# Crossing the second pair of each first matrix, and adding the first sum of two pairs per later group on VectorE

## The chip, the cores and the metric

One core of a Trainium2 chip runs the kernel. The metric is the device time of one execution in microseconds. Before the change the median of three runs is 1181.12 us (1180.35 to 1185.26).

## What is computed

The reference is a two-layer encoder on 512 tokens of width 1024, with 16 learned tokens put in front (528 in all). What matters here is the MLP that ends each layer:

```python
def sq_relu_mlp(y, w_up, w_down):
    u = y @ w_up                                  # 1024 -> 4096
    return jnp.square(jax.nn.relu(u)) @ w_down    # 4096 -> 1024

for i in range(DEPTH):                            # DEPTH = 2
    y = rmsnorm(h, norm_gains[i, 0])
    y = mlstm_mixer(y, ...) if i % 2 == 0 else diff_attention(y, ...)
    h = h + y
    h = h + sq_relu_mlp(rmsnorm(h, norm_gains[i, 1]), mlp_w_up[i], mlp_w_down[i])
h = rmsnorm(h, final_gain)
```

Everything is float32. The MLP of layer 0 works on 528 tokens, that of layer 1 on 512.

## The kernel before

Activations lie transposed in SBUF, features on the 128 partitions and tokens along the row. Each float32 factor is split in a hi part (ScalarE copies it to the type of TensorE's operands) and a lo part (VectorE subtracts the hi part from the original), and each product is three matmuls: hi x hi, hi x lo, lo x hi.

The MLP's 4096 inner features are cut in four groups. A group has eight *pairs*; a pair is 256 output columns of a weight matrix, loaded as one transfer of 1 MB to `raw[:, i % 2]` by SyncE. Pairs 0 to 3 of a group are columns of `w_up` (their output is relu'd, squared and kept in `ah`, `al`), pairs 4 to 7 are columns of `w_down`. So i counts 0 to 31 in a layer.

A *plain* pair is two blocks of 128 columns, each with eight slices of the inner dimension: 96 matmuls of 264 columns in layer 0, 48 of 512 in layer 1. A *crossed* pair is a two-by-two block product with seven products instead of eight (Winograd's form). The weights' forms are S1 = A21 + A22, S2 = S1 - A11, S3 = A22 - S2, S4 = A12 - S2; the tokens' forms are kept in `th`, `tl`, made once at the start of a layer's MLP by `forms_hi` (ScalarE) and `forms_lo` (VectorE). The seven products A11, A12, S1, S2, S4, S3, A22 take 12 matmuls each. In between ScalarE copies the results of A11, S1 and S2 out of PSUM (`snap` P1, P5, U2), since their banks are added to by later products, and VectorE adds them back in two sums (`total` C22 and C1). S2's product waits for the copy P1, S4's for P5, S3's for U2, A22's for C22. `pe_order` writes the order of the products: the last product of a pair, A22, comes after A11 and S1 of the next one.

`crossed(i)` says which pairs are crossed. With PLAIN = 2, pairs 0 and 1 of the first matrix are plain, all other pairs of the first matrix and all `w_up` pairs of the later groups are crossed, and so are the last three `w_down` pairs of all groups but the last.

S1 needs a sum of two quarters of `raw`. GpSimd makes it (`weight_sum`, L741) by a DMA of 256 KB that reads the quarter from HBM again and accumulates it on the one in `raw`, after the 1 MB load has landed. The forms S2, S3, S4 are three VectorE instructions on 512 columns (`form`, L1734); their hi part is `form_hi`, their lo part `form_lo` (L1741); hi and lo parts of what is taken from `raw` as it is are `natural_hi` and `natural_lo` (L1747) in crossed pairs, `plain_hi` and `plain_lo` (L1686) in plain ones, with m = 0 for the first half and m = 1 for the second, which holds S1 and A22.

At the start of the MLP VectorE also refines the norm's factor (`refine_factor`, L1809 to L1811), and scales the residual in four pieces (`scale_residual`, L1801), which GpSimd saves to HBM (`h_sum`), since the squares overwrite `h`. `squares` is on ScalarE (L1116, L1117), the lo part of its result, `act_lo`, on VectorE (L1771).

Every engine's order is written out by hand in a loop over i; all of them take their work in order, and wait on semaphores that count what has been done. `READY`, `DONE`, `COPIED`, `ADDED` are tables of these counts. SyncE loads pair i when the lo part m = 1 of pair i - 2 is made (L626).

Of the kernel before, what the change touches and what calls it, by code (L numbers as in the profile page):

```python
# [72 lines left out]
PLAIN = 2  # L73
# [18 lines left out]
def sent_down(i):  # L92

    return 0 <= i < PAIRS - 8 and i % 8 >= 4

# [25 lines left out]
def counted(things):  # L121
# [7 lines left out]
RANK = counted(i for i in range(PAIRS) if crossed(i))  # L129
# [6 lines left out]
N_DONE, N_READY, N_TAKEN, N_OUT, N_CROSSED, N_COPIED, N_ADDED, N_SENT = (  # L136
    len(x) for x in (DONE, READY, TAKEN, SENT_OUT, RANK, COPIED, ADDED, SENT))
# [97 lines left out]
def program(nc, a, out):  # L235
    with ExitStack() as ctx:
# [275 lines left out]
        def raw_summed(layer, i):  # L512

            crosses = [k for k in range(i % 2, PAIRS, 2) if crossed(k)]
            return m_sum[i % 2], 16 * (len(crosses) * layer + crosses.index(i) + 1)
# [47 lines left out]
        def _(sp):  # L563
# [96 lines left out]
        def _(pool):  # L660
# [69 lines left out]
            def residuals(layer):  # L730
# [18 lines left out]
                for q in range(4):  # L749
                    if q % 2 == 0:  # L750
                        weight_sum(PLAIN + q // 2)
                    pool.wait_ge(h_scaled, FACTOR * layer + q + 3)
                    pool.dma_start(h_sum[2 * q:2 * q + 2, :, t0:T].rearrange("k p t -> p k t"),
                                   h[:, 2 * q:2 * q + 2, t0:T]).then_inc(h_saved[q // 2], 16)
                for q in range(2):
                    pool.wait_ge(h_saved[q], 32 * (layer + 1))
                for i in range(PAIRS - 7):
                    if sent_down(i):
                        send_sum(i, 0)
                        send_sum(i, 1)  # L760
                    if i + 3 > PLAIN + 1 and crossed(i + 3):
                        weight_sum(i + 3)
# [44 lines left out]
        def _(act):  # L807
# [249 lines left out]
            def mlp(layer, spans):  # L1057
                t0, w = mlp_shape(layer)
                mid = t0 + w
                items, ranks, norm = layer * N_DONE, layer * N_CROSSED, 2 * layer + 1  # L1060
                copies, adds = layer * N_COPIED, layer * N_ADDED

                def form_hi(i, group):

                    act.wait_ge(s_made, 3 * (ranks + RANK[i] - 1) + (2 if group == "S23" else 3))
                    act.wait_ge(m_done, items + last_use(i, "S3" if group == "S23" else "S4"))
                    rows = slice(8, 16) if group == "S23" else slice(16, 20)
                    copy(hi[1 - i % 2][:, rows, :], lof[1 - i % 2][:, rows, :]).then_inc(m_hi, 1)

                def natural_hi(i, m):  # L1070

                    act.wait_ge(*(raw_summed if m else raw_landed)(layer, i))
                    act.wait_ge(m_done, items + last_use(i, "A22" if m else "A12"))
                    copy(hi[1 - i % 2][:, slots(i, m), :], raw[:, i % 2, :, P * m:P * m + P]).then_inc(m_hi, 1)
# [26 lines left out]
                def squares(i, m):  # L1101
# [3 lines left out]
                    if i > 0:  # L1105
                        positive(i, m)
# [56 lines left out]
                for i in range(PAIRS):  # L1163
                    if i == 0:
                        plain_hi(layer, 1, 0)
                        plain_hi(layer, 1, 1)
# [10 lines left out]
                    if begins:  # L1177
                        snap(i, "P1")
                        if i == PLAIN:
                            squares(1, 0)  # L1180
                        else:
# [9 lines left out]
                    if i == PLAIN:  # L1191
                        squares(1, 1)
                    if first_down:
                        block_hi(i, "A22")
                    if crossed(i + 1) and not first_down and i != PLAIN:
                        natural_hi(i + 1, 1)
                    if crossed(i) and is_up(i) and not begins:
                        snap(i, "U2")
# [3 lines left out]
                    if i > 1 and not in_tail(layer, i - 1) and not sent_down(i - 1) and not (sent_down(i) and i % 8 == 4) and not begins and not last_row:  # L1202
# [25 lines left out]
                    if i == 1:  # L1228
                        squares(0, 0)
                        squares(0, 1)  # L1230
                    if i >= PAIRS - 4 and not in_tail(layer, i):
                        finish(i, 0)
                    if first_down:
                        snap(i + 1, "P1")
                        snap(i + 1, "P5")
                        finish(i, 0)
                    elif crossed(i):
                        if i == PLAIN:
# [196 lines left out]
        def _(dve):  # L1435
# [280 lines left out]
            def mlp(layer, spans):  # L1716
                t0, w = mlp_shape(layer)
                mid = t0 + w
                items, ranks, norm = layer * N_DONE, layer * N_CROSSED, 2 * layer + 1
                copies, adds, t_in = layer * N_COPIED, layer * N_ADDED, spans[0][0]  # L1720

                def form(i, name, after):

                    made = 3 * (ranks + RANK[i] - 1)
# [5 lines left out]
                    if name == "S2":  # L1730
                        dve.wait_ge(*raw_summed(layer, i))
                    wait(dve, s_made, after and made + after)
                    dve.wait_ge(m_done, items + last_use(i, name))
                    V.tensor_tensor(f[:, out_rows, :], x, y, ALU.subtract).then_inc(s_made, 1)  # L1734

                def form_lo(i, group):

                    dve.wait_ge(s_made, 3 * (ranks + RANK[i]))
# [14 lines left out]
                def total(i, name):  # L1753
# [6 lines left out]
                    else:  # L1760
                        dve.wait_ge(m_done, items + DONE[i, "S3"])
                        dve.wait_ge(p_copied, copies + COPIED[i, "P5"])
                        dve.wait_ge(*freed(layer, i - 2, 1))
# [40 lines left out]
                def refine_factor():  # L1804

                    made, ms, r = FACTOR * layer + 1, ab[1][:, t_in:T], rb[:, t_in:T]
# [37 lines left out]
                for i in range(PAIRS):  # L1844
                    if i == 0:
                        plain_lo(layer, 1, 0)
                        plain_lo(layer, 1, 1)
                        refine_factor()
                        for n in range(4):
                            forms_lo(n)  # L1850
                        scale_residual(0)
                        scale_residual(1)
# [8 lines left out]
                    if crossed(i + 1):  # L1861
# [10 lines left out]
                    if crossed(i + 1):  # L1872
# [261 lines left out]
        def _(pe):  # L2134
# [228 lines left out]
            def mlp(layer, spans):  # L2363
                t0, w = mlp_shape(layer)
                mid = t0 + w
                items, ranks, norm = layer * N_DONE, layer * N_CROSSED, 2 * layer + 1
# [21 lines left out]
                def plain_waits(i, m):  # L2388
# [4 lines left out]
                    else:  # L2393

                        pe.wait_ge(evac, u_out + (5 if (i, m) == (0, 0) else 8))
                        if (i, m) == (1, 1):
                            pe.wait_ge(ln_done, norm + 1)

                def product(i, name):
# [8 lines left out]
                    if name in ("A11", "S1", "A12"):  # L2408
                        pe.wait_ge(*freed(layer, i - 2, int(name == "A11")))
                    elif name == "A22":  # L2410
# [303 lines left out]
```

## Time and profile before

| | |
|---|---|
| median of three runs | 1181.12 us |
| profiled execution | 1185.41 us |
| its span, first to last instruction | 1183.6 us |
| TensorE busy | 1170.5 us, 99% |
| VectorE busy | 947.8 us, 80% |
| ScalarE busy | 794.7 us, 67% |
| GpSimd busy | 176.7 us, 15% |
| granted TensorE clock | 0.999 of full speed |
| moved by DMA | 143.83 MB, mean 122 GB/s |

The MLP of layer 0 runs from about 251 to 590 us of the span, that of layer 1 from about 837 us to near the end. Busy times are those of instructions; a wait shows as idle time before an instruction, with what ended it.

### The profile page before, as it was taken

What the parts mean: (1) busy time and instruction counts of PE and PEld (TensorE: products, weight loads), DVE (VectorE), ACT (ScalarE), POOL (GpSimd) and SP (SyncE); (2) the same over time, 40 slices, a digit from 0 to 9 for tenths busy, and PEclk for the clock granted to TensorE, in tenths of its full rate; (3) what the DMA queues carried; (4) which work ended last, traced back from release to release, by engine and by line L of the source; (5) the groups of instructions that cost most, each with busy time, mean ns of one, the idle gap of its engine ahead of it and who ended that gap; (6) DMA issues with size and microseconds to landing.
All of it is one profiled execution on the core that took longest, in us unless ns stands there. A gap on an engine that the chain in (4) does not pass through costs nothing.

```text
span 1183.6 us, 23240 instructions
## 1 busy us (share of the span) xinstructions
PE 1170.5 (99%) x8881; PEld 1125.1 (95%) x8881; DVE 947.8 (80%) x1441; ACT 794.7 (67%) x1401; POOL 176.7 (15%) x215
## 2 busy tenths in 40 slices
PE   9999999999999999999999999999999999999998
PEld 8999999999999999999999999987799899999987
DVE  6889888778977878775578889887988788797764
ACT  5777877756667667666357887887576676766753
POOL 3221120001220220222020000000103103113100
PEclk9999999999999999999999999999999999999999
DMA  7343332335694793884132122213458748759722
GB/s 180 95 104 95 89 98 90 93 100 163 146 187 125 137 195 99 175 198 141 55 96 66 55 71 71 89 37 92 129 157 166 167 102 181 156 135 185 195 75 72
DMA packets 176634, 143.83 MB, mean 122 GB/s; under 512 B 23913, under 2 KB 167329, under 8 KB 176545
## 3 DMA queue, kind: packets, MB, share of 16 engines
q1 hardware_dynamic: 141600, 104.93, 30.1%
q0 software_dynamic: 34816, 37.59, 18.6%
q8 instruction: 60, 0.98, 0.3%
q14 instruction: 30, 0.24, 0.1%
q10 hardware_dynamic: 128, 0.09, 0.0%
HBM read 123.42 MB, written 19.17 MB: 120 GB/s over the span
## 4 chain that ended last, share of the span: by engine, by line
PE 76%; issue 17%; DMA 4%; DVE 2%; ACT 1%; POOL 1%; DVEq 0%; POOLq 0%; ACTq 0%
PE ps L2433 36%; PE ps L2148 18%; PE ps L2383 14%; DMA raw<-in_mlp_w_up_dram 3%; PE ps L2652 2%; PE ps L2203 1%; PE ps L2221 1%; PE ps L2335 0%; PE ps L2300 0%; DMA meta_in<-in_meta_tokens_dram 0%; PE ps L2289 0%; DVE lo L1747 0%; DVE blocks_f L1787 0%; ACT wh L809 0%; POOL qm L794 0%
## 5 line engine op out<-in xcount | busy, mean ns | idle before, releaser
L809 ACT ACTIVATE hi<-raw 128x1024 fp32r<-128x1024 f32 x128 | 133.5, 1050 | 44.3 <-PE ps L2383 20.0
L2148 PE MATMUL ps<-yh,wh 128*128 128x264 f32 (+1 forms) x704 | 160.6, 302 | 0.0
L2148 PE MATMUL ps<-yl,wh 128*128 128x264 f32 (+1 forms) x704 | 155.3, 295 | 0.0
L2148 PE MATMUL ps<-yh,wl 128*128 128x264 f32 (+1 forms) x704 | 155.3, 295 | 0.0
L2433 PE MATMUL ps<-th,hi 128*128 128x264 f32 (+1 forms) x448 | 127.3, 284 | 3.7 <-ACT pu L809 2.8
L2433 PE MATMUL ps<-tl,hi 128*128 128x264 f32 (+1 forms) x448 | 126.5, 282 | 0.0
L2433 PE MATMUL ps<-th,lo 128*128 128x264 f32 (+1 forms) x448 | 126.5, 282 | 0.0
L1747 DVE TENSOR_TENSOR lo<-raw,hi 128x1024 fp32r<-128x1024 f32 x92 | 112.2, 1220 | 5.4 <-ACT hi L809 4.9
L2433 PE MATMUL ps<-yl,hi 128*128 128x264 f32 (+1 forms) x408 | 115.7, 284 | 0.0
L2433 PE MATMUL ps<-yh,hi 128*128 128x264 f32 (+1 forms) x408 | 115.3, 283 | 0.0
L2433 PE MATMUL ps<-yh,lo 128*128 128x264 f32 (+1 forms) x408 | 115.1, 282 | 0.0
L2148 PEld LDWEIGHTS ps<-yh,wh 128*128 128x128 f32 x704 | 112.0, 189 | 2.9 <-DVE yl L1448 0.4
L2148 PEld LDWEIGHTS ps<-yh,wl 128*128 128x128 f32 x704 | 111.1, 188 | 2.8
L2148 PEld LDWEIGHTS ps<-yl,wh 128*128 128x128 f32 x704 | 111.3, 188 | 1.6
L1741 DVE TENSOR_TENSOR lo<-lof,hi 128x1024 fp32r<-128x1024 f32 x92 | 86.9, 952 | 4.0 <-ACT hi L809 4.0
L2433 PEld LDWEIGHTS ps<-th,hi 128*128 128x128 f32 x448 | 84.4, 188 | 5.3 <-ACT pu L809 3.4
L809 ACT ACTIVATE hi<-lof 128x1024 fp32r<-128x1024 f32 x92 | 73.6, 836 | 21.0 <-DVE lof L1734 20.2
L1441 DVE TENSOR_TENSOR wl<-raw,wh 128x1024 fp32r<-128x1024 f32 x64 | 78.2, 1222 | 9.4 <-ACT wh L809 8.0
L2433 PEld LDWEIGHTS ps<-tl,hi 128*128 128x128 f32 x448 | 84.4, 188 | 0.0
L2433 PEld LDWEIGHTS ps<-th,lo 128*128 128x128 f32 x448 | 84.3, 188 | 0.0
L2433 PE MATMUL ps<-al,hi 128*128 128x264 f32 (+1 forms) x288 | 81.6, 283 | 0.0
L2433 PE MATMUL ps<-ah,hi 128*128 128x264 f32 (+1 forms) x288 | 81.5, 283 | 0.0
(332 smaller groups left out, 3463.4 us busy)
## 6 DMA issues: line engine op xcount, KB each, us to landing
raw<-in_mlp_w_up_dram SPq DMA_DIRECT2D x32, 1024.0 KB, 6.5
raw<-in_mlp_w_down_dram SPq DMA_DIRECT2D x32, 1024.0 KB, 5.5
raw<-in_diff_w_in_dram SPq DMA_DIRECT2D x24, 512.0 KB, 3.7
raw<-in_mlstm_w_in_dram SPq DMA_DIRECT2D x16, 512.0 KB, 4.4
raw<-in_mlp_w_up_dram POOLq DMA_DIRECT2D x28, 256.0 KB, 7.2
h_sum<-abuf POOLq DMA_DIRECT2D x24, 264.0 KB, 5.8
h_sum<-abuf POOLq DMA_DIRECT2D x24, 256.0 KB, 6.5
raw<-in_mlp_w_down_dram POOLq DMA_DIRECT2D x18, 256.0 KB, 5.0
```

The lines of the kernel that those rows point to most:

```text
L809: return nc.scalar.activation(o, i, ACT.Copy, scale=scale)
L1441: V.tensor_tensor(wl[:, k, :, :], raw[:, k // 2, :, P * (k % 2):P * (k % 2) + P], wh[:, k, :, :].bitcast(F32), ALU.subtract).then_inc(spli ...
L1741: V.tensor_tensor(lo[1 - i % 2][:, rows, :], lof[1 - i % 2][:, rows, :], hi[1 - i % 2][:, rows, :].bitcast(F32), ALU.subtract).then_inc(m_ ...
L1747: V.tensor_tensor(lo[1 - i % 2][:, slots(i, m), :], raw[:, i % 2, :, P * m:P * m + P], hi[1 - i % 2][:, slots(i, m), :].bitcast(F32), ALU. ...
L2148: last = mm(ps[:, bank + s, 0:w_], w[:, slot, kb, :], m[:, kb, t0:t0 + w_], start=(kb == 0 and n == 0), stop=(kb == CB - 1 and n == 2))
L2203: last = mm(ps[:, b, c:c + t1 - t0], what(j), p, start=(b not in seen), stop=(n == 1 and i == len(passes) - 1))
L2221: last = mm(ps[0:rows, b, c:c + t1 - t0], ks[par][:, s0:s0 + rows], q[:, t0:t1], start=(m == 0), stop=(m == 1))
L2383: last = mm(ps[:, b + s, 0:cw], x[half][:, 20 * m + kb, :], y[:, kb, c0:c0 + cw], start=(kb == 0 and n == 0), stop=(kb == CB - 1 and n == 2))
L2433: last = mm(ps[:, bank, 0:w], x[1 - i % 2][:, at, :], y, start=(kb == 0 and n == 0 and name in ("A11", "S1", "A12")), stop=(kb == 3 and n ...
L2652: last = mm(ps[:, j % 2, 0:XH], x[half][:, 20 * m + kb, :], y[:, kb, c0:c0 + XH], start=(kb == 0 and n == 0), stop=(kb == CB - 1 and n == 2))
```

## The change

PLAIN becomes 1: pair 1 of the first matrix is crossed as well. In pairs 0 and 1 of the later groups (i = 8, 9, 16, 17, 24, 25) VectorE adds the first sum itself (`own_sum`), and `weight_sum` is left out for them. The counts on the semaphore of the forms become a table, MADE. The order of the work at the start is rewritten on ScalarE and VectorE. Cut to its core:

```diff
-PLAIN = 2
+PLAIN = 1
+def summed_here(i):
+    return crossed(i) and i >= 8 and i % 8 < 2
-RANK = counted(i for i in range(PAIRS) if crossed(i))
+MADE = counted((i, n) for i in range(PAIRS) if crossed(i) for n in ("S1", "S2", "S3", "S4") if n != "S1" or summed_here(i))
 # SyncE, the load of pair i
-    sp.wait_ge(m_lo, layer * N_READY + READY[i - 2, "S1A22" if crossed(i - 2) else 1])
+    sp.wait_ge(m_lo, layer * N_READY + READY[i - 2, ("S23" if i - 2 == PLAIN + 1 else "S1A22") if crossed(i - 2) else 1])
 # GpSimd
 for q in range(4):
-    if q % 2 == 0:
-        weight_sum(PLAIN + q // 2)
-    pool.wait_ge(h_scaled, FACTOR * layer + q + 3)
+    if q == 0:
+        weight_sum(1)
+        weight_sum(2)
+    if q == 2:
+        weight_sum(3)
+    pool.wait_ge(h_scaled, FACTOR * layer + q + 1)
...
-        if i + 3 > PLAIN + 1 and crossed(i + 3):
+        if i + 3 > 3 and crossed(i + 3) and not summed_here(i + 3):
             weight_sum(i + 3)
 # ScalarE, loop over i
 if i == 0:
-    plain_hi(layer, 1, 0)
-    plain_hi(layer, 1, 1)
+    natural_hi(1, 0)
     norm_factor(norm, spans)
...
-if i == 1:
-    squares(0, 0)
-    squares(0, 1)
...
+elif i == PLAIN:
+    snap(i + 1, "P1")
+    snap(i + 1, "P5")
+    squares(0, 0)
+    squares(0, 1)
+    snap(i + 1, "U2")
+    positive(1, 0)
+    positive(1, 1)
+    natural_hi(i + 2, 1)
+    squares(1, 0)
+    squares(1, 1)
 elif crossed(i):
-    if i == PLAIN:
+    finish(i, 0)
+    if crossed(i + 1):
         snap(i + 1, "P1")
-    finish(i, 0)
-    if crossed(i + 1) and i != PLAIN:
-        snap(i + 1, "P1")
-    if crossed(i + 1):
         snap(i + 1, "P5")
 # VectorE
+def own_sum(i):
+    dve.wait_ge(*raw_landed(layer, i))
+    s1 = raw[:, i % 2, first_k(i), P:2 * P]
+    V.tensor_tensor(s1, s1, raw[:, i % 2, second_k(i), P:2 * P], ALU.add).then_inc(s_made, 1)
...
 if i == 0:
-    plain_lo(layer, 1, 0)
-    plain_lo(layer, 1, 1)
-    refine_factor()
+    natural_lo(1, 0)
+    form(1, "S2")
+    form(1, "S3")
+    form(1, "S4")
     for n in range(4):
         forms_lo(n)
-    scale_residual(0)
-    scale_residual(1)
...
-if crossed(i + 1):
+if crossed(i + 1) and i != PLAIN:
     natural_lo(i + 1, 1)
...
-if crossed(i + 1):
+if crossed(i + 1) and i != PLAIN:
     form_lo(i + 1, "S23")
...
 if i == PLAIN:
-    for n in range(4):
-        act_lo(n // 2, n % 2)
-elif i > 1 and is_up(i - 1) and not sent_down(i):
+    form_lo(i + 1, "S23")
+if i > 1 and is_up(i - 1) and not sent_down(i):
     act_lo(i - 1, 1)
...
+if i == 1:
+    scale_residual(2)
+    scale_residual(3)
...
 if crossed(i + 2):
+    if i == 0:
+        scale_residual(0)
+        scale_residual(1)
     if not (sent_down(i) and i % 8 == DOWN_FROM - 1):
         natural_lo(i + 2, 0)
-    form(i + 2, "S2", 0)
-    form(i + 2, "S3", 1)
-    form(i + 2, "S4", 1)
     if i == 0:
-        scale_residual(2)
-        scale_residual(3)
+        natural_lo(2, 1)
+    if summed_here(i + 2):
+        own_sum(i + 2)
+    form(i + 2, "S2")
+    form(i + 2, "S3")
+    form(i + 2, "S4")
+    if i == 1:
+        act_lo(0, 0)
+        act_lo(0, 1)
+        refine_factor()
```

So on VectorE the order from the start of the MLP to the second lo part of pair 3 is: lo (1,0), forms of pair 1, four `tl`, lo (1,1), both form lo parts of pair 1, two scalings, lo (2,0), lo (2,1), forms of pair 2, C22 and C1 of pair 1, both form lo parts of pair 2, two scalings, lo (3,0), forms of pair 3, `al` of pair 0 twice, the factor, lo (3,1). After it come `al` (1,0), the first form lo part of pair 3, C22 and C1 of pair 2. On ScalarE a pair's first two squares now stand before the next pair's P1 from pair 2 on.

## Rows read from the trace of the kernel before

**Rows 1.** The page's busy times, TensorE: busy, share of span, instructions.

```profile
PE 1170.5 (99%) x8881; PEld 1125.1 (95%) x8881; DVE 947.8 (80%) x1441; ACT 794.7 (67%) x1401; POOL 176.7 (15%) x215
```

**Rows 2.** Waits of TensorE over the span: us in total, times, longest us.

```profile
PE ps L2433 <- ACT pu L809: 2.8, 2, 2.1
...
PE ps L2433 <- DVE lo L1747: 0.6, 1, 0.6
```

**Rows 3.** The chain of waits: start us, us, what, instructions.

```profile
257.73 17.53 PE ps L2383 x144
275.26 20.45 PE ps L2433 x168
...
503.71 8.74 DMA raw<-in_mlp_w_up_dram
...
837.50 5.59 PE ps L2383 x24
...
860.66 18.44 PE ps L2433 x156
...
922.61 8.68 DMA raw<-in_mlp_w_up_dram
```

**Rows 4.** Timeline of TensorE at two waits: start, duration, line, shape, idle before.

```profile
513.87 0.39 PE L2433 MATMUL ps<-th,hi 128*128 128x264 f32 x1 [0.66 <-ACT pu L809]
...
932.69 0.39 PE L2433 MATMUL ps<-th,hi 128*128 128x256 f32 x1 [2.11 <-ACT pu L809]
```

**Rows 5.** Timeline of VectorE, the first form of pair 25 in layer 0.

```profile
512.48 0.69 DVE L1734 TENSOR_TENSOR lof<-raw 128x512 f32<-128x512 f32 x1 [5.05 <-DMA raw<-in_mlp_w_up_dram]
```

**Rows 6.** Busy time in a window: TensorE, its loads, VectorE, ScalarE, GpSimd, clock, DMA.

```profile
262.00:278.00 16.00, 16.00 (x133) 16.00 (x133) 15.97 (x17) 10.46 (x16) 4.25 (x5) 1.00 0.71 205
```

**Rows 7.** Timeline of VectorE at the start of layer 0's MLP.

```profile
259.83 0.71 DVE L1809 SCALAR_TENSOR_TENSOR acc<-abuf,rb 128x528 f32<-128x528 f32 x1 [0.37 <-ACT rb L846]
...
261.32 4.76 DVE L1842 TENSOR_TENSOR tl<-tf,th 128x1056 fp32r<-128x1056 f32 x4
266.00 2.42 DVE L1801 TENSOR_TENSOR h<-h,abuf 128x1056 f32<-128x1056 f32 x2
268.34 1.22 DVE L1747 TENSOR_TENSOR lo<-raw,hi 128x1024 fp32r<-128x1024 f32 x1
269.47 0.69 DVE L1734 TENSOR_TENSOR lof<-raw 128x512 f32<-128x512 f32 x1
...
271.40 2.42 DVE L1801 TENSOR_TENSOR h<-h,abuf 128x1056 f32<-128x1056 f32 x2
...
274.88 1.82 DVE L1741 TENSOR_TENSOR lo<-lof,hi 128x1024 fp32r<-128x1024 f32 x2
276.62 1.22 DVE L1747 TENSOR_TENSOR lo<-raw,hi 128x1024 fp32r<-128x1024 f32 x1
...
285.44 0.43 DVE L1765 TENSOR_TENSOR ps<-ps,p 128x264 f32<-128x264 f32 x1
285.78 0.71 DVE L1765 TENSOR_TENSOR ps<-ps,pu 128x528 f32<-128x528 f32 x1
286.39 2.56 DVE L1771 TENSOR_TENSOR al<-blocks_f,ah 128x528 fp32r<-128x528 f32 x4
```

**Rows 8.** Timeline of ScalarE at the start of both MLPs.

```profile
259.70 4.00 ACT L809 ACTIVATE th<-tf 128x1056 fp32r<-128x1056 f32 x4
...
290.18 0.61 ACT L1099 ACTIVATE tbuf<-ps 128x528 f32<-128x528 f32 x1
...
291.90 1.99 ACT L809 ACTIVATE hi<-raw 128x1024 fp32r<-128x1024 f32 x2
...
845.83 3.89 ACT L809 ACTIVATE th<-tf 128x1024 fp32r<-128x1024 f32 x4
```

**Rows 9.** The page's DMA issues: times, size, median us to landing.

```profile
raw<-in_mlp_w_up_dram SPq DMA_DIRECT2D x32, 1024.0 KB, 6.5
...
raw<-in_mlp_w_up_dram POOLq DMA_DIRECT2D x28, 256.0 KB, 7.2
```

More of the change, by code:

```diff
@@ L512, in raw_summed @@
         def raw_summed(layer, i):
-            crosses = [k for k in range(i % 2, PAIRS, 2) if crossed(k)]
+            crosses = [k for k in range(i % 2, PAIRS, 2) if crossed(k) and not summed_here(k)]
             return m_sum[i % 2], 16 * (len(crosses) * layer + crosses.index(i) + 1)
@@ L1059, in mlp @@
                 mid = t0 + w
[L1060 removed]
+                items, made, norm = layer * N_DONE, layer * N_MADE, 2 * layer + 1
                 copies, adds = layer * N_COPIED, layer * N_ADDED
                 def form_hi(i, group):
[L1065 to L1066 removed]
+                    act.wait_ge(s_made, made + MADE[i, "S3" if group == "S23" else "S4"])
+                    if i > 1:
+                        act.wait_ge(m_done, items + last_use(i, "S3" if group == "S23" else "S4"))
                     rows = slice(8, 16) if group == "S23" else slice(16, 20)
@@ L1178, in mlp @@
                         snap(i, "P1")
-                        if i == PLAIN:
-                            squares(1, 0)
-                        else:
+                        if not is_up(i):
                             block_hi(i, "S3")
@@ L1190, in mlp @@
                         snap(i, "U2")
-                    if i == PLAIN:
-                        squares(1, 1)
                     if first_down:
                         block_hi(i, "A22")
-                    if crossed(i + 1) and not first_down and i != PLAIN:
+                    if crossed(i + 1) and not first_down and not 1 <= i <= 2:
                         natural_hi(i + 1, 1)
-                    if crossed(i) and is_up(i) and not begins:
+                    if crossed(i) and is_up(i) and not begins and i != 2:
                         snap(i, "U2")
@@ L1201, in mlp @@
                     last_row = i > PAIRS - 4 and not in_tail(layer, i - 1)
-                    if i > 1 and not in_tail(layer, i - 1) and not sent_down(i - 1) and not (sent_down(i) and i % 8 == 4) and not begins and not last_row:
+                    if i > 2 and not in_tail(layer, i - 1) and not sent_down(i - 1) and not (sent_down(i) and i % 8 == 4) and not begins and not last_row:
                         finish(i - 1, 1)
@@ L1718, in mlp, with form @@
                 mid = t0 + w
-                items, ranks, norm = layer * N_DONE, layer * N_CROSSED, 2 * layer + 1
+                items, made, norm = layer * N_DONE, layer * N_MADE, 2 * layer + 1
                 copies, adds, t_in = layer * N_COPIED, layer * N_ADDED, spans[0][0]
-                def form(i, name, after):
-                    made = 3 * (ranks + RANK[i] - 1)
+                def own_sum(i):
+                    dve.wait_ge(*raw_landed(layer, i))
+                    s1 = raw[:, i % 2, first_k(i), P:2 * P]
+                    V.tensor_tensor(s1, s1, raw[:, i % 2, second_k(i), P:2 * P], ALU.add).then_inc(s_made, 1)
+                def form(i, name):
                     r, f = raw[:, i % 2, :, :], lof[1 - i % 2]
@@ L1729, in form @@
                     x, y = {"S2": (s1, a11), "S3": (a22, f[:, 8:12, :]), "S4": (a12, f[:, 8:12, :])}[name]
-                    if name == "S2":
+                    if name != "S2":
+                        dve.wait_ge(s_made, made + MADE[i, "S2"])
+                    elif summed_here(i):
+                        dve.wait_ge(s_made, made + MADE[i, "S1"])
+                    else:
                         dve.wait_ge(*raw_summed(layer, i))
-                    wait(dve, s_made, after and made + after)
-                    dve.wait_ge(m_done, items + last_use(i, name))
+                    if i > 1:
+                        dve.wait_ge(m_done, items + last_use(i, name))
+                    else:
+                        dve.wait_ge(unit_done, (U_OUT0, U_OUT1)[layer] + 8)
                     V.tensor_tensor(f[:, out_rows, :], x, y, ALU.subtract).then_inc(s_made, 1)
                 def form_lo(i, group):
-                    dve.wait_ge(s_made, 3 * (ranks + RANK[i]))
+                    dve.wait_ge(s_made, made + MADE[i, "S4"])
                     dve.wait_ge(m_hi, layer * N_READY + READY[i, group])
@@ L1804, in refine_factor @@
                 def refine_factor():
-                    made, ms, r = FACTOR * layer + 1, ab[1][:, t_in:T], rb[:, t_in:T]
+                    made, ms, r = FACTOR * layer + 5, ab[1][:, t_in:T], rb[:, t_in:T]
                     p = acc[:, t_in:T]
@@ L2365, in mlp @@
                 mid = t0 + w
-                items, ranks, norm = layer * N_DONE, layer * N_CROSSED, 2 * layer + 1
+                items, made, norm = layer * N_DONE, layer * N_MADE, 2 * layer + 1
                 ready, copies, adds = layer * N_READY, layer * N_COPIED, layer * N_ADDED
```

29 lines of the change are left out of this document (19 added, 10 removed).

## The prediction

> **What bounds the kernel now.** I read the page's busy shares first: TensorE is busy 1170.5 of 1183.6 us [rows 1], so time is gained by giving it less to do, or lost by making it wait. The table of waits, for TensorE alone, comes next: the only waits inside the two MLPs that come to anything are 2.8 us on copies to `pu` by ScalarE and 0.6 us on a `lo` by VectorE [rows 2]. The chain of waits says what lies behind them: near 504 and near 923 us it runs through a transfer to `raw`, 8.74 and 8.68 us long, the accumulating DMA that forms the first sum of a pair; elsewhere it is TensorE's own run of matmuls [rows 3]. The timeline of TensorE places the two copies: 0.66 us before 513.87, 2.11 us before 932.69, both an S3 product waiting for U2 in pair 24 or 25, the first of the last group [rows 4]. ScalarE's copy was late because the hi part of the next pair's sum stands ahead of it, and that sum had not landed; VectorE sat idle 5.05 us for the same sum before 512.48 [rows 5].
>
> The reader should then look at the start of layer 0's MLP on VectorE. From 262 to 278 us it is busy 15.97 of 16.00 us [rows 6], though nothing waits for it. That is where the change puts more work.
>
> **Fewer matmuls (the second pair crossed).** A plain pair is 96 matmuls of 264 columns, a crossed one 7 products of 12. 144 plain ones take 17.53 us, 0.1217 each; 168 crossed ones 20.45 us, 0.1217 each [rows 3]. Twelve fewer: -1.46 us in layer 0. In layer 1 a plain pair is 48 matmuls of 512 columns, 24 in 5.59 us, so 11.17 us; crossed matmuls of 256 take 18.44/156 = 0.118, so 9.93 to 9.97 with the few short gaps; -1.2 us. Together -2.65 us if TensorE never waits.
>
> **What it asks of VectorE.** Pair 1 now needs S2, S3, S4, their two lo parts, and C22 and C1, where a plain pair needs none. The prices are the distances between starts [rows 7]: the three forms 1.93 (269.47 to 271.40), two form lo parts 1.74 (274.88 to 276.62), C22 0.34, C1 0.61. That is 4.6 us more VectorE work, in a stretch that was full, and pair 3's lo part is due 1.46 us sooner.
>
> I write out the new order in layer 0, up to the lo part of pair 3's S1 and A22. ScalarE makes `th` from 259.70 in four pieces of 1.00 [rows 8], so VectorE can start `tl` at about 260.8; the lo part of raw of pair 1 and its three forms (1.13 + 1.93) stand before that and wait only for a hi part that ScalarE makes ahead of the norm's factor; they fill a hole and cost nothing. Then, without a hole: four `tl` 4.68 (261.32 to 266.00); lo parts of raw, (1,1), (2,0), (2,1), (3,0), (3,1), five of 1.13 = 5.65; form lo parts of pairs 1 and 2, 3.48; four residual scalings of 1.17 = 4.68; forms of pairs 2 and 3, 3.86; C22 and C1 of pair 1, 0.95; two `al` of 0.62 = 1.24 (2.56 for four, overlapped a little); refining the factor 1.49 (259.83 to 261.32, with its second half) [rows 7]. Sum 26.03, so 286.8 us.
>
> TensorE comes there as follows. Pair 1 starts at 257.73 + 48 x 0.1217 = 263.57 [rows 3]. S1 of pair 3 is the fifteenth product, 14 x 1.46 later, 284.0 us. Small waits on the way: S1 of pair 1 for the lo part that ends at 266.6 (0.1 to 0.2), S2 of pair 1 for the P1 copy (0.1 to 0.2), S2 of pair 2 for P1, which now follows the hi part of raw 3 on ScalarE (0.3). So S1 is asked for at 284.6 and starts at 286.9: a wait of 2.3 us. Behind it in VectorE's order stand `al` (1,0) 0.62, the form lo of pair 3 1.14, C22 of pair 2 0.34, ready at 289.0; A22 of pair 2 is asked for at 288.4, 0.6 us more. C1 is made at 289.6; ScalarE then does pair 2's relu and two squares before it copies P1 of pair 3 (290.18 to 291.90 is 1.72 for those, and a copy is 0.3 [rows 8]): 291.65. S2 of pair 3 starts at 291.7, another 1.2 us. In the kernel before it starts at 275.26 + 9 x 1.46 = 288.4 [rows 3]. So layer 0 loses 3.3 us net of the saved matmuls. From there TensorE sets the pace again, and a delay is not caught up, because it had no holes to give.
>
> Layer 1 is the same list: `th` starts at 845.83 in pieces of 0.95 [rows 8], VectorE from 846.9 with 25.7 us of work (its pieces of 256 columns are shorter, as 3.89 against 4.00 for the four `th` shows) ends at 872.6. Pair 1 starts at 860.5 - 11.17 = 849.3, and product fifteen is due 14 x 1.425 later, 869.3, with 0.9 of small waits 870.2. A wait of 2.4, then 0.6 and 1.2 as before; S2 of pair 3 at 877.4 against 860.5 + 12.8 = 873.3. Net loss 4.1 us. Both layers: +7.4 us. Bounds: if TensorE never waited -2.65; if every piece comes as listed and the third matrix or its sum lands late as well, up to +12 (third rival).
>
> **The first sums on VectorE (pairs 8, 9, 16, 17, 24, 25 of each layer).** Twelve additions of 128x512, nearest row the form of the same shape, 0.69 us [rows 5]. At pair 25 the addition stands where VectorE idled 5.05 us, so it is covered; without cover each would cost at most 0.7, 8 us in all, but VectorE is not late in those groups. Twelve accumulating DMAs go and two come (pair 1). GpSimd's queue gets shorter: it holds `h_sum` sends and the later sums alone, which can only come earlier. The raw load of pair 4 now waits for the form lo of pair 2 instead of the S1/A22 lo; 277 against 274 us or so, and it is not needed for ten more. What it gives back is the 2.8 + 0.6 = 3.4 us of waits [rows 2], in the profiled execution. Lower bound 0, where the sums land in time anyway.
>
> On this the Trainium skill speaks against the change: its page "DMA: Bandwidth & Descriptors", section "Anatomy of one DMA — SWDGE (gpsimd) path", fits about 2.0 us plus bytes over 436e3 to a DMA issued from GpSimd, an estimate of 2.6 us for the 256 KB here. By it no sum would be late, and this part would be worth 0 instead of 3.4. The trace has 8.74 us for the one at 503.71, with a load of 1 MB and the sends beside it [rows 3], and that decides.
>
> **Copies ahead of squares.** Moving P1, P5 of pair 2 ahead of squares of pair 0 costs ScalarE nothing: squares of pair 0 are asked for by `al` only after 283 us. Its price is inside the sum above.
>
> **The sum.** The profiled execution took 1185.41 us in all, 1.8 beyond its span, and 4.3 more than the median 1181.12; two of the three runs shown lie at 1180.35 and 1181.12, one at 1185.26. On the profiled execution: 1185.4 + 7.4 - 3.4 = 1189.4. The distance from the profiled execution to the median is about the size of the late-sum waits, so a median run may hold few of them; between 0 and 3.4 removable I take 2.5, since the transfers are the same in every run and the waits come from them. 1181.1 + 7.4 - 2.5 = **1186.0 us**.
>
> **Rivals.**
> 1. VectorE is not late at pair 3 in fact: the small pieces overlap more, or the early work runs ahead. For it: nothing waited for VectorE there before. Against: 15.97 of 16.00 busy [rows 6]. Then only the gains stay: -2.65 and -2.5 to -3.4, 1175.0 to 1176.0. It decides if `lo` of pair 3 starts before 283 us. Chance 0.08.
> 2. Only the first wait appears: C22 and P1 of the next pair come on time, since VectorE has caught up one piece. That takes away 1.8 us per layer: 1182.4. For it: 288.4 against 289.0 is close. Against: both are in-order queues behind the late piece. Chance 0.18.
> 3. The load of pair 3 is issued only after the lo part of S1/A22 of pair 1, about 266.7 instead of 259.5, into the two `h_sum` saves. Median landing of such a load is 6.5 us and of a sum 7.2 [rows 9]; 266.7 + 6.5 + 7.2 = 280.4, and the forms of pair 3 are reached at 281.1. Two or three us more and VectorE stands still at that form with `lo` (3,1) behind it: +2 us a layer, 1190. Chance 0.12.
>
> The forecast has 0.62, own range 1183 to 1190, half of it above 1187.0. About 0.5% (5.9 us) is what a measurement of this kernel tells from no change. Slower: 0.31 + 0.11 = 0.42. Faster: 0.08. Within: 0.50. Range 1179 to 1190.5, which leaves out the first rival and half of the third.
>
> **What would show it.** Right: in both layers a wait of TensorE of 2 to 2.5 us on VectorE's `lo<-raw` some 23 us after the MLP's second plain block, with VectorE without a hole before it; then a wait of about 0.6 on its `ps` addition and about 1.2 on the copy to `pu`; no DMA of `raw` in the chain at the last group's start. The crossed products count 84 matmuls more in each layer, the plain blocks 96 fewer in layer 0 and 48 fewer in layer 1. Wrong: no wait there, or one that a DMA ends; or waits that stay at 24 and 25, now on VectorE's addition.

## The result and the profile after

The changed kernel takes 1187.17 us (median of seven, 1186.90 to 1187.55), the kernel before 1182.17 us in its seven (1179.66 to 1185.26). The ratio is 1.0042, with a 95% interval of 1.0033 to 1.0052: slower by about 5 us. The profiled executions are 1187.55 and 1185.41 us, only 2.1 us apart, because the profiled execution of before was slower than all of its seven runs.

The table of waits of TensorE after the change, for the MLPs' products (us in total, times, longest us), answers to [rows 2]:

```profile
PE ps L2472 <- DVE lo L1775: 4.8, 4, 2.1
PE ps L2472 <- ACT pu L817: 2.1, 2, 1.0
...
PE ps L2472 <- DVE ps L1794: 1.0, 2, 0.5
```

TensorE's timeline places them (start, duration, line, shape, idle before and what ended it). These are S1 of pair 3, A22 of pair 2 and S2 of pair 3, in layer 0 and again in layer 1:

```profile
287.08 0.39 PE L2472 MATMUL ps<-th,hi 128*128 128x264 f32 x1 [2.10 <-DVE lo L1775]
...
289.28 0.36 PE L2472 MATMUL ps<-th,hi 128*128 128x264 f32 x1 [0.46 <-DVE ps L1794]
...
292.02 0.36 PE L2472 MATMUL ps<-th,hi 128*128 128x264 f32 x1 [1.04 <-ACT pu L817]
...
874.77 0.39 PE L2472 MATMUL ps<-th,hi 128*128 128x256 f32 x1 [2.15 <-DVE lo L1775]
...
876.95 0.36 PE L2472 MATMUL ps<-th,hi 128*128 128x256 f32 x1 [0.49 <-DVE ps L1794]
...
879.63 0.36 PE L2472 MATMUL ps<-th,hi 128*128 128x256 f32 x1 [1.04 <-ACT pu L817]
```

The same three waits, 2.1, 0.5 and 1.0 us, stand in both layers. The table's other two waits on `lo` are smaller ones, 0.25 and 0.34 us, at S1 of pair 1. The matmul ahead of the first began at 284.70, so from there to 287.08 start to start it costs 2.26 us more than the 0.12 between two matmuls.

VectorE from the start of its list to C1 of pair 2, which answers to [rows 7] (x4 and the like: instructions run together in one row):

```profile
260.90 4.76 DVE L1871 TENSOR_TENSOR tl<-tf,th 128x1056 fp32r<-128x1056 f32 x4 [0.49 <-ACT th L817]
...
281.16 0.68 DVE L1762 TENSOR_TENSOR lof<-raw 128x512 f32<-128x512 f32 x1
...
284.33 0.70 DVE L1838 SCALAR_TENSOR_TENSOR acc<-abuf,rb 128x528 f32<-128x528 f32 x1
...
285.80 1.22 DVE L1775 TENSOR_TENSOR lo<-raw,hi 128x1024 fp32r<-128x1024 f32 x1
286.95 0.70 DVE L1800 TENSOR_TENSOR al<-blocks_f,ah 128x528 fp32r<-128x528 f32 x1
...
288.70 0.43 DVE L1794 TENSOR_TENSOR ps<-ps,p 128x264 f32<-128x264 f32 x1
289.04 0.70 DVE L1794 TENSOR_TENSOR ps<-ps,pu 128x528 f32<-128x528 f32 x1
```

`tl` starts at 260.90 and lo (3,1), the piece of 285.80, is followed at 286.95. That is 26.05 us of work without a hole: no row between the first and lo (3,1) has idle time before it. In layer 1 the same list runs from 848.95 to 874.64, 25.69 us. What follows it is late in order: `al`, the form lo part, C22 at 288.70, C1 at 289.04. ScalarE then does pair 2's relu and squares and only then the copy to `pu` of which S2 has need, at 291.51 (answers to [rows 8]):

```profile
290.97 0.63 ACT L1134 ACTIVATE ah<-tbuf 128x528 fp32r<-128x528 f32 x1
291.51 0.37 ACT L817 ACTIVATE pu<-ps 128x264 f32<-128x264 f32 x1
```

The other half of the change shows in the chain of waits. Products run without a break from pair 5 of one group to pair 3 of the next, seven times 84 = 588 matmuls, in three such runs per layer. After, each is one piece:

```profile
311.50 71.75 PE ps L2472 x588
...
394.90 71.74 PE ps L2472 x588
...
478.30 71.76 PE ps L2472 x588
...
898.68 69.86 PE ps L2472 x588
...
979.70 69.75 PE ps L2472 x588
...
1060.60 69.75 PE ps L2472 x588
```

Before, from the first row of such a run to the plain matmuls behind it; here the first run of layer 0 and that of layer 1:

```profile
307.65 38.19 PE ps L2433 x312
...
379.99 11.65 PE ps L2383 x96
...
892.23 15.99 PE ps L2433 x132
...
965.99 11.15 PE ps L2383 x48
```

These took 379.99 - 307.65 = 72.34 us and 965.99 - 892.23 = 73.76. All six, read in this way, were 72.34, 71.76, 72.95, 73.76, 69.76 and 70.04 us before and 71.74, 71.74, 71.76, 69.86, 69.74 and 69.74 after: 6.0 us of the profiled execution of before are gone.

The books close. From the start of block (0,1) of pair 0 to the first plain matmul of pair 4, layer 0 took 257.37 to 295.55 before and 257.52 to 299.40 after, +3.70 us; layer 1 took 843.39 to 880.34 and 845.44 to 886.81, +4.42. Together +8.12, less 6.0, is +2.1, and the two profiled executions differ by 2.14.

### The profile page after: what moved, and what is told of

It reads as the page before. It is cut to its first block, busy times and chain, and to the rows that moved or that the text cites. A ratio compares the mean times of both kernels' runs of the same rounds, so it can differ in the third digit from the quotient of the medians.

```text
span 1185.8 us, 23342 instructions
## 1 busy us (share of the span) xinstructions
PE 1168.3 (99%) x8905; PEld 1124.6 (95%) x8905; DVE 965.6 (81%) x1467; ACT 796.9 (67%) x1411; POOL 163.2 (14%) x205
## 4 chain that ended last, share of the span: by engine, by line
PE 74%; issue 17%; DVE 5%; ACT 2%; POOL 1%; DMA 0%; DVEq 0%; POOLq 0%; ACTq 0%
PE ps L2472 37%; PE ps L2186 18%; PE ps L2421 11%; PE ps L2691 2%; PE ps L2241 1%; PE ps L2259 1%; DVE lo L1775 1%; ACT hi L817 1%; DVE h L1830 1%; ACT th L817 1%; DVE lof L1762 1%; DVE lo L1769 1%; PE ps L2373 0%; PE ps L2338 0%; DMA meta_in<-in_meta_tokens_dram 0%
## 5 line engine op out<-in xcount | busy, mean ns | idle before, releaser
L2472 PE MATMUL ps<-th,hi 128*128 128x264 f32 (+1 forms) x480 | 136.6, 285 | 7.9 <-DVE lo L1775 4.8
L2472 PE MATMUL ps<-tl,hi 128*128 128x264 f32 (+1 forms) x480 | 135.5, 282 | 0.0
L2472 PE MATMUL ps<-th,lo 128*128 128x264 f32 (+1 forms) x480 | 135.5, 282 | 0.0
L2472 PE MATMUL ps<-yl,hi 128*128 128x264 f32 (+1 forms) x432 | 122.5, 283 | 0.0
L2472 PE MATMUL ps<-yh,hi 128*128 128x264 f32 (+1 forms) x432 | 122.1, 283 | 0.0
L2472 PE MATMUL ps<-yh,lo 128*128 128x264 f32 (+1 forms) x432 | 121.9, 282 | 0.0
L2472 PEld LDWEIGHTS ps<-th,hi 128*128 128x128 f32 x480 | 90.4, 188 | 10.0 <-DVE lo L1775 5.7
L2472 PEld LDWEIGHTS ps<-tl,hi 128*128 128x128 f32 x480 | 90.4, 188 | 0.0
L2472 PEld LDWEIGHTS ps<-th,lo 128*128 128x128 f32 x480 | 90.3, 188 | 0.0
L2472 PEld LDWEIGHTS ps<-yl,hi 128*128 128x128 f32 x432 | 81.3, 188 | 0.9 <-DVE lo L1769 0.5
```

The lines of the kernel that those rows point to most:

```text
L2472: last = mm(ps[:, bank, 0:w], x[1 - i % 2][:, at, :], y, start=(kb == 0 and n == 0 and name in ("A11", "S1", "A12")), stop=(kb == 3 and n ...
```

## Experiments

Each kernel was timed in five rounds against the kernel before on the same chip. Times are medians. Ratios are to the kernel before beside it; differences to the changed kernel are between medians taken on different occasions; the one kernel timed twice, on two chips, came out 0.26 us apart. "Start" is the stretch from block (0,1) of pair 0 to pair 4.

### The sums back on GpSimd

```diff
 def summed_here(i):
-    return crossed(i) and i >= 8 and i % 8 < 2
+    return False
```

> The changed kernel with all first sums made by GpSimd's accumulating DMAs again; the second pair stays crossed. Theory (late sums cost 0 to 3.4 us, the rest of the change costs 7.4): the waits at the first pairs of the last group come back, on the copy U2 behind the hi part of the sum, 1187.2 plus 2.0 to 3.4, so 1189 to 1190.5 us, ratio to before 1.006 to 1.007. Rival (the sums were late only in the profiled execution of before): 1187.2 within 0.4, with a spread as small as that of the changed kernel. The waits at pair 3 (2.1, 0.5, 1.0 us in each layer) stay the same in both.

Measured 1191.15 us (1190.34 to 1193.34), ratio 1.0062 (1.0043 to 1.0082), 4.0 us more than the changed kernel (3.2 more, if each is set against the kernel before beside it). The start keeps its three waits: 2.3, 0.6 and 1.2 us start to start. The chain of waits goes again through accumulating DMAs, in the first and in the third run of layer 0:

```profile
329.12 9.63 DMA raw<-in_mlp_w_up_dram
...
506.88 9.06 DMA raw<-in_mlp_w_up_dram
```

Ahead of each stands the 1 MB load that it waits for, 7.87 us from 320.97 and 8.52 from 498.02. The theory of late sums holds, and its size was low: 4.0 us, not 2 to 3.4. The length of the six runs shows it: 72.71, 72.05, 72.40, 71.07, 70.28 and 70.32 us, 4.2 more in all than the 424.6 after. The place was expected only in part: the longest additions are in the first run of each layer, not in the last, and of the 4.2 us the table of waits lists 0.9 on copies to `pu`; the rest is distances of 0.2 to 0.4 us between matmuls, most with no wait listed. The rival falls.

### The sums on VectorE alone

```diff
+def own_sum(i): ...            # and summed_here, MADE, as in the change; PLAIN stays 2
+                        if summed_here(i + 2):
+                            own_sum(i + 2)
                         form(i + 2, "S2", 0)
```

> The kernel before with VectorE adding the first sum of pairs 0 and 1 of the later groups, and nothing else changed. Theory: faster than before by what the late sums cost, about 2.5 us of the median (0 to 3.4), 1179 to 1180 us, ratio 0.997 to 0.9985, and its runs spread less than the 5 us of before, since no product waits for an accumulating DMA there. Rival (the twelve additions load VectorE enough to cost something, 12 x 0.7 at most): no faster, 1182 or more.

Measured 1179.15 us (1178.97 to 1180.67), ratio 0.9963 (0.9950 to 0.9976); the 26 runs of before beside it have a median of 1182.93 and run from 1180.53 to 1188.60. The rival (the additions cost something) falls: the six runs take 71.74 to 71.76 and 69.74 to 69.88 us, as in the changed kernel. A second timing of the same kernel on another chip:

> The kernel before with only the sums on VectorE, again, on the same chip as the best order of the crossed pair: 1179.15 within 0.3. The difference to the other kernel of this call is what the second crossed pair is worth with its order repaired: 1.5 us by the theory (2.65 of matmuls less about 1.1 of waits and restarts), nothing by the rival (the saved matmuls come back as waits whatever the order).

gave 1179.41 us, ratio 0.9983 (0.9974 to 0.9992), against 1181.98 for before; its eleven runs go from 1178.89 to 1180.75 us. TensorE's table of waits has nothing of the products; of the MLPs, one of 0.3 us at a plain product of layer 1 stays, which is in the changed kernel too:

```profile
PE ps L2403 <- DVE al L1789: 0.3, 1, 0.3
```

This half is worth 2.6 to 3.8 us, and the spread is smaller: eight of the first nine runs lie within 0.33 us and the ninth 1.4 above them, and the second timing spans 1.9 us, where the kernel before spans 8.1 in 26 runs. The changed kernel is 8.0 us slower than this one; that is the price of the crossed pair and its order.

### VectorE's pieces of no hurry moved behind C1

```diff
@@ VectorE, i == 1
-                        if i == 1:
-                            act_lo(0, 0)
-                            act_lo(0, 1)
-                            refine_factor()
@@ VectorE, i == 2, before the form lo part
-                    if up_before and not sent_down(i):
+                    if up_before and not sent_down(i) and i != 2:
                         act_lo(i - 1, 0)
@@ after total(i, "C1")
+                    if i == 2:
+                        act_lo(0, 0)
+                        act_lo(0, 1)
+                        act_lo(1, 0)
+                        refine_factor()
```

> The changed kernel with the lo parts of the squares of pair 0 (two), of pair 1 (one) and the refining of the factor moved on VectorE from ahead of lo (3,1), C22 and C1 of pair 2 to behind them; nothing is left out. Theory (VectorE's in-order work of 26 us makes lo (3,1) late): lo (3,1) starts 2.7 us earlier, no wait at S1 of pair 3; A22 of pair 2 waits 0 to 0.3; C1 comes at about 287.1, so S2 of pair 3 still waits about 1.2 us for P1 behind the relu and the squares. Gain about 2.6 us a layer, 1182.0 us, ratio 1.000. Rival (the load of pair 3 or its sum is what comes late): lo (3,1) is held by its hi part, and S1 still waits over 1 us; gain under 1 us a layer.

Measured 1182.33 us (1182.06 to 1182.63), ratio 0.9988 (0.9978 to 0.9999): 4.8 us less than the changed kernel, 5.2 expected. lo (3,1) starts at 282.87 instead of 285.80 (0.22 of that is an earlier start of the MLP, so 2.7 us as expected), with no hole before it, and no wait at S1 is left. The start is 2.43 us shorter in layer 0 and 2.41 in layer 1, as much as the medians. The load of pair 3 and its sum were in time:

```profile
282.87 1.22 DVE L1775 TENSOR_TENSOR lo<-raw,hi 128x1024 fp32r<-128x1024 f32 x1
284.91 1.23 DVE L1769 TENSOR_TENSOR lo<-lof,hi 128x1024 fp32r<-128x1024 f32 x1 [0.82 <-ACT hi L817]
286.05 0.43 DVE L1794 TENSOR_TENSOR ps<-ps,p 128x264 f32<-128x264 f32 x1
```

VectorE now waits 0.82 us for ScalarE's hi part of the form, so C22 comes at 286.05; A22 and S2 wait in TensorE's timeline:

```profile
286.63 0.36 PE L2473 MATMUL ps<-th,hi 128*128 128x264 f32 x1 [0.41 <-DVE ps L1794]
...
289.38 0.36 PE L2473 MATMUL ps<-th,hi 128*128 128x264 f32 x1 [1.04 <-ACT pu L817]
```

The first wait was VectorE's list. The second shrank by 0.05 us only, since ScalarE's two squares of pair 1 stand ahead of that hi part.

### P1 ahead of pair 2's squares

```diff
 elif crossed(i):
+    if i == 2:
+        snap(i + 1, "P1")
     finish(i, 0)
     if crossed(i + 1):
-        snap(i + 1, "P1")
+        if i != 2:
+            snap(i + 1, "P1")
```

> The changed kernel with ScalarE's copy P1 of pair 3 put ahead of the relu and the squares of pair 2 (m = 0). Theory (the third wait is ScalarE's order behind a late C1): the wait of 1.0 us at S2 of pair 3 goes in both layers and the first two stay, gain about 2.4 us, 1184.8 us, ratio 1.002. Rival (C1 itself comes too late for S2): the wait shrinks to half at most, gain under 1 us.

Measured 1186.14 us, ratio 1.0025 (1.0012 to 1.0037), in a wide spread: three of twelve runs at 1184.48 to 1184.51, the others up to 1187.97. The profiled run is one of the three, and there the third wait is gone and the first two stand:

```profile
PE ps L2475 <- DVE lo L1778: 4.8, 4, 2.1
...
PE ps L2475 <- DVE ps L1797: 1.0, 2, 0.5
```

In this trace the start is 1.24 us shorter in layer 0 and 1.33 in layer 1. The three runs meet the 1184.8 expected; the median gives only 1.0 us. The nine longer runs had a mean granted clock of 0.994 to 0.997, the three 0.998 and 0.999. There is no trace of a longer one, so that the clock made them longer is not shown; the changed kernel's own runs at 0.996 (1187.03 and 1187.17 us) are no longer than its others. What a stretch at the lower clock costs is in the next experiment, and the size of this move rests on that one.

### Both moves

```diff
@@ both edits above together
```

> The changed kernel with both earlier edits together: VectorE's four late-needed pieces behind C1 of pair 2, and P1 of pair 3 ahead of pair 2's relu and squares. The first alone measured 4.8 us less than the changed kernel, the second removed 1.2 us a layer in its trace. Theory (three independent terms of one lateness): no wait at S1 and S2 of pair 3, A22 of pair 2 still waits 0.4 us for C22; 1187.2 - 4.8 - 2.4 = 1180.0 us, ratio 0.997. Rival (a wait that is removed only shifts to the next item): the P1 copy taken away leaves a wait elsewhere, and the two together give under 6 us, above 1181.3.

Measured 1180.04 us, ratio 0.998 (0.997 to 0.999); 1180.0 was expected. Taking P1 out of the way is worth 1182.33 - 1180.04 = 2.3 us, as its wait said. No wait moved elsewhere; of the three what is left is 0.42 and 0.49 us at A22. Ten of twelve runs lie between 1179.70 and 1180.31 us, two are at 1181.51 and 1181.52. The profiled run is one of those two, and its windows (us; busy time of TensorE, its weight loads, VectorE, ScalarE and GpSimd; granted clock; DMA share; GB/s) show where its 1.5 us are, at the beginning of the execution, far from the change:

```profile
10.00:12.00 2.00, 0.00 (x0) 0.02 (x1) 1.97 (x8) 1.68 (x3) 0.00 (x0) 1.00 1.15 313
12.00:14.00 2.00, 1.99 (x10) 1.79 (x11) 2.00 (x4) 1.75 (x3) 0.77 (x1) 0.52 1.09 328
14.00:16.00 2.00, 2.00 (x13) 1.88 (x12) 1.95 (x4) 1.45 (x4) 1.25 (x2) 0.62 1.22 290
16.00:18.00 2.00, 2.00 (x20) 1.97 (x19) 1.30 (x3) 2.00 (x4) 1.86 (x2) 1.00 1.17 192
```

TensorE had waited 2.01 us there for the load of `xin`, and then ran for some 3.4 us at the lower of its two clock levels, 1.2 instead of 2.4 GHz. That load was no later than elsewhere: the matmul behind it started at 12.01 us, and at 11.80 to 12.20 in the other profiles, where TensorE reached it with waits of at most 0.68 us and the clock did not fall. Block (0,1) of pair 0 starts at 258.53 us here and at 256.91 to 257.52 there.

### Squares ahead of the copies

```diff
+                        squares(0, 0)
+                        squares(0, 1)
                         snap(i + 1, "P1")
                         snap(i + 1, "P5")
-                        squares(0, 0)
-                        squares(0, 1)
                         snap(i + 1, "U2")
```

> The changed kernel with ScalarE's squares of pair 0 (2.2 us) put back ahead of the copies P1 and P5 of pair 2; nothing is left out. Theory (VectorE's list sets when S1 of pair 3 starts, whatever TensorE does before): a new wait of about 2.0 us at S2 of pair 2 on the copy to pu, the wait on lo (3,1) shrinks from 2.1 to nearly nothing, S1 of pair 3 starts within 0.3 us of where it did, and the time is 1187.2 within 0.6. Rival (waits of TensorE add up): about 2 us more a layer, 1191 us.

Measured 1187.62 us, ratio 1.0038 (1.0025 to 1.0052), 0.45 us more than the changed kernel, where 1191 was the other answer. S2 of pair 2 now waits 2.02 us for its copy, and S2 of pair 3, of the old waits, 0.49:

```profile
279.37 0.36 PE L2472 MATMUL ps<-th,hi 128*128 128x264 f32 x1 [2.02 <-ACT pu L817]
...
291.81 0.36 PE L2472 MATMUL ps<-th,hi 128*128 128x264 f32 x1 [0.49 <-ACT pu L817]
```

After the first of these the granted clock was at the lower level through most of two windows, which delayed TensorE by another 1.5 us (15 matmuls at 0.22 us start to start instead of 0.12):

```profile
280.00:282.00 2.00, 2.00 (x13) 2.00 (x12) 1.97 (x3) 0.57 (x2) 0.71 (x1) 0.63 1.09 403
282.00:284.00 2.00, 2.00 (x11) 2.00 (x10) 2.00 (x4) 2.00 (x4) 0.00 (x0) 0.52 1.00 371
284.00:286.00 2.00, 2.00 (x19) 2.00 (x18) 1.93 (x4) 2.00 (x5) 0.00 (x0) 1.00 0.06 19
```

Neither cost anything in layer 0. Its start took 41.89 us (257.30 to 299.19), the changed kernel's 41.88; in layer 1, where the wait was 2.08 us and the clock fell too, it took 41.55 against 41.37. TensorE now came to lo (3,1) late enough not to wait. As long as VectorE is late, what delays TensorE ahead of it is free, and "copies first" is worth nothing there. VectorE's list sets the end of this stretch.

### One more VectorE piece

```diff
-FACTOR = 6
+FACTOR = 7
...
+                    V.tensor_tensor(p, ms, r, ALU.mult).then_inc(h_scaled, 1)
+                    dve.wait_ge(h_scaled, made - 1)
                     V.scalar_tensor_tensor(p, ms, -1.0, r, ALU.mult, ALU.mult).then_inc(h_scaled, 1)
```

> The changed kernel with one more VectorE piece of 128x528 (128x512 in layer 1), 0.7 us, ahead of lo (3,1): the factor's first product is made twice. Theory (VectorE's list is the bound there): the wait at S1 of pair 3 grows by 0.72 in each layer, the others stay, 1187.2 + 1.45 = 1188.6 us, ratio to before 1.0055. Rival (the list has a hole, or the hi part sets lo (3,1)): the wait and the time stay within 0.4 us.

Measured 1189.22 us (1188.95 to 1190.23), ratio 1.0053 (1.0038 to 1.0069), 2.05 us more than the changed kernel where 1.45 was expected. In layer 0 the first wait grew from 2.10 to 2.85 us, the two others did not:

```profile
287.46 0.39 PE L2474 MATMUL ps<-th,hi 128*128 128x264 f32 x1 [2.85 <-DVE lo L1775]
...
289.66 0.36 PE L2474 MATMUL ps<-th,hi 128*128 128x264 f32 x1 [0.46 <-DVE ps L1794]
...
292.41 0.36 PE L2474 MATMUL ps<-th,hi 128*128 128x264 f32 x1 [1.05 <-ACT pu L817]
```

The start took 42.64 us in layer 0 and 42.11 in layer 1, where the changed kernel took 41.88 and 41.37: +0.76 and +0.74 for a piece of 0.7 us, which is the list's signature. The two profiled executions differ by 1.40 us, as expected. The medians differ by 0.65 more, and the mean granted clock of these six runs was 0.995 to 0.998. In layer 1 the clock fell after the wait of 2.86 us:

```profile
874.00:876.00 2.00, 0.00 (x0) 0.00 (x0) 1.93 (x4) 0.75 (x1) 0.00 (x0) 1.00 0.00 0
876.00:878.00 2.00, 1.94 (x12) 1.93 (x12) 2.00 (x4) 0.00 (x0) 0.00 (x0) 0.74 0.36 95
878.00:880.00 2.00, 2.00 (x10) 1.79 (x9) 2.00 (x5) 1.25 (x3) 0.00 (x0) 0.50 1.06 375
880.00:882.00 2.00, 1.93 (x15) 1.76 (x14) 1.62 (x2) 1.05 (x3) 0.00 (x0) 0.91 0.18 62
```

There it filled the waits at A22 and S2, of which only 0.07 us is listed in that layer, and so cost nothing; a fall in a place without such cover costs about 1.5 us, as above. That this is what lengthened the other five runs is not shown.

### C22 early, and the hi part before a pair of squares

```diff
@@ on top of both moves; VectorE
+                    if i == 2:
+                        total(i, "C22")
                     if crossed(i + 1) and i != PLAIN:
                         form_lo(i + 1, "S23")
@@ ScalarE
                     if crossed(i + 1):
                         form_hi(i + 1, "S23")
+                    if i == 2:
+                        squares(1, 1)
...
                         squares(1, 0)
-                        squares(1, 1)
```

> As the two moves together, and C22 of pair 2 put ahead of the form lo part of pair 3, with the hi part of that form ahead of ScalarE's second squares of pair 1. Theory: the wait at A22 of pair 2 goes too (0.5 us a layer), so of the new waits only those of 0.3 us at S1 of pair 1 are left: 1179.0 us, ratio 0.996, within 0.5 us of the kernel that has only the sums on VectorE (1179.15), because what remains of the saved matmuls (2.65) is lost in waits that the chain from the block norm sets (about 1 us a layer). Rival (the second crossed pair is worth its 2.65 us once VectorE's order lets it): 1177 us or less.

Measured 1178.47 us (1178.23 to 1179.88), ratio 0.9965 (0.9953 to 0.9978): the fastest median here. 1179.0 was expected, and 1177 or less by the rival, which falls. All three new waits are gone in both layers; only those at S1 of pair 1 stay:

```profile
PE ps L2479 <- DVE lo L1779: 0.6, 2, 0.3
...
PE ps L2428 <- DVE al L1804: 0.3, 1, 0.3
```

The two edits were made together, so what each of them is worth alone is not shown.

### The lo part of pair 1 earlier

```diff
@@ on top of the last; ScalarE, and the same on VectorE with forms_lo, natural_lo
-                        for n in range(4):
-                            forms_hi(n)
+                        forms_hi(0)
+                        forms_hi(1)
+                        natural_hi(1, 1)
+                        forms_hi(2)
+                        forms_hi(3)
...
```

> As the kernel with the two moves and the early C22 (1178.5 us), and the hi and lo part of pair 1's S1 and A22 put between the second and the third of the four hi and lo parts of the tokens' forms. Theory (the wait at S1 of pair 1 is the same in-order lateness: the lo part stands behind four tl, of which S1 needs one): lo (1,1) is ready 2.3 us earlier, the waits of 0.25 and 0.34 us at S1 of pair 1 go, 1178.5 - 0.9 = 1177.6 us, ratio 0.996. Rival (another piece takes its place: the third tl or the form lo of pair 1 comes late for S2 or S3): no gain, 1178.3 to 1178.7.

Measured 1178.74 us, ratio 0.9972 (0.9963 to 0.9981): no gain. S1 of pair 1 no longer waits, and the next product, S2, waits 0.50 us for the form lo part, twice what S1 had waited:

```profile
268.52 0.36 PE L2485 MATMUL ps<-th,hi 128*128 128x264 f32 x1 [0.50 <-DVE lo L1776]
```

The theory was wrong here and the rival right. ScalarE and VectorE have as much to do as before between the norm's factor and S2 of pair 1, in whatever order; that no order at all would do better is argued, not shown. On the same chip the sums alone gave 1179.41, so the second crossed pair, in the best order found, is worth 0.7 us of its 2.65, where 1.5 was expected. The traces put all of it in layer 0: the start takes 37.53 us there against 38.19, and 36.96 against 36.95 in layer 1.

## Why the prediction was right

**TensorE bounds, and has no holes.** Right for the change as made: every wait that came is in the time, as the sum of the two sections shows (+8.12 - 6.0 = +2.1 on the profiled executions).

**Fewer matmuls, -2.65 us.** Right as far as the traces tell: the matmul instructions are 24 more (8905 against 8881), since 168 crossed ones replace 96 in layer 0 and 48 wide ones in layer 1. Of the time only 0.7 us is left even in the best order found, because the crossed pair's products restart after small gaps. In layer 0 of the kernel with C22 early, distances of 0.53, 0.23, 0.25, 0.20, 0.18 and 0.20 us stand at S1 and S2 of pair 1 and S2 of pair 2 (266.25 to 277.05) where 0.12 is the rule, 0.87 us over it; in layer 1 they come to 1.1 us, about all that was saved there.

**VectorE's list, 26.03 us.** Right to 0.02 us (26.05), and not by errors that cancel: each kind of piece in it is met within 0.05 us. Layer 1's 25.7 came out as 25.69. Expected starts in layer 0 were 286.9 for S1, 289.0 for A22 and 291.7 for S2; measured 287.08, 289.28 and 292.02, of which 0.15 is that the MLP began later. The waits were expected as 2.3, 0.6 and 1.2 and cost 2.26, 0.63 and 1.20 start to start. Three experiments show the cause: 2.7 us of work out of the way removes the first wait, 0.7 us more of it lengthens the wait by 0.75, and 3.5 us of delay to TensorE ahead of it change nothing in layer 0.

**Net price of the start, 7.4 us.** Slightly low: 8.1 in the traces, 8.0 between the changed kernel and the one with the sums alone. The difference is in restarts. The second matmul behind each of the three waits comes after 0.19 to 0.23 us instead of 0.12, 0.5 us in the two layers, which I had put at nothing; and the small waits ahead of them came to 0.9 and 1.1 us where I had 0.6 and 0.9.

**The late sums.** The mechanism was right, the size was the weak term. I read 3.4 us from the table of waits and took 2.5 for the median run; the profiled execution had 6.0, and removing them is worth 4.0 us in the changed kernel (3.2 against the kernels before beside them) and 2.6 to 3.8 in the kernel before. The mis-sized term is the 2.5 us: a table of waits leaves out small gaps between matmuls, which only the length of a run of products counts. In the sum the two errors work against each other, 0.6 us too little on the price and 0.1 to 1.3 too little on the gain: +4.9 us was forecast and +5.0 measured, which is closer than the terms deserve, and that is luck. The 1.17 us between 1186.0 and 1187.17 are nearly all the kernel before, which I took at the 1181.12 us of three runs and which has 1182.17 in seven.

The rule of the Trainium skill, page "DMA: Bandwidth & Descriptors", section "Anatomy of one DMA — SWDGE (gpsimd) path", would have given 2.6 us per sum, an estimate by its fit, and nothing to gain. The accumulating DMAs in the chains took 9.63 and 9.06 us with the sums back on GpSimd, and 8.74 before; the shortest of the 48 in the MLPs of that run took 4.4. The part was worth 4.0 us; the trace decides.

**Rivals.** The first (VectorE is not late) is excluded by its own sign, since lo (3,1) starts at 285.80 and not before 283, and by the one more piece. The second (only the first wait) by the traces: 0.46 and 1.04 us stand. The third (the load of pair 3 late) did not come: the load was issued at 266.83, as foreseen, but took 5.65 us and its sum, issued at 272.77, 4.54, so the sum had landed at 277.3, and the forms of pair 3 start at 281.16 with no idle time before them.

## What to carry to other kernels

When an in-order engine is busy in every slice of a stretch, write out its list from the last true dependency to the next item that the bound engine needs, and add up the distances between starts; here that sum was exact to 0.02 us while the table of waits of the kernel before said that nothing waited. Put pieces that are not due soon (here the lo parts of pair 0's squares, made at 283.1 and read from 299.4 on) behind those with one before paying for a cheaper product. And measure what late transfers cost by the length of the stretch against a clean one, not by the listed waits.

## What the runs showed of the hardware

With the first sums of pairs 0 and 1 of the later groups on VectorE, instead of by GpSimd DMAs that accumulate 256 KB, the run times spread by 1.7 and 1.9 us (nine and eleven runs) where the kernel before spread by 8.1 (1180.53 to 1188.60 in 26 runs). Not every kernel with these sums on VectorE is that steady: the one with P1 ahead ran from 1184.48 to 1187.97.

I had not expected the clock to matter. In three profiles it fell from 2.4 to 1.2 GHz for some 3.4 us after TensorE had waited: after 2.01 us at the beginning of one, after 2.02 in layer 0 and 2.08 in layer 1 of another, after 2.86 in layer 1 of the third. It did not always fall: the changed kernel's waits of 2.10 and 2.15 us and one of 2.85 left it at 1.00, and so did one of 2.11 before the change, two with the sums back on GpSimd and two with P1 ahead (2.11 to 2.14). One fall cost 1.5 us where nothing covered it (1181.52 against 1180.0 us) and nothing where a late engine lay behind it. Such a wait can thus cost more than its length, but the clock fell after four of these twelve only, and the profiles do not show what decides.
